# Two weight blocks in one walk over the normed tiles, and four quarter products moved ahead of the first scores

## The chip, the cores and the metric

The kernel runs on one core of one Trainium2 chip. The metric is the device time of one execution in microseconds (us); lower is better.

## The reference, cut to what matters

The program computes a mixer block with five branches and then a second block of two layers. The change sits in the first layer of the second block, an mLSTM over 512 tokens of 1024 features, 8 heads, float32:

```python
hn = rmsnorm(x, norm1_w[layer]) * (1 + scale1) + shift1
proj = h @ w_in
qk = jax.nn.silu(causal_conv(proj[..., :2 * M_QK], conv_w, conv_b))
v, o = ...                      # values and output gate, 1024 columns each
i_pre = IGATE_CAP * jnp.tanh(i_pre / IGATE_CAP)      # 8 columns of proj, one a head
lf = jax.nn.log_sigmoid(f_pre)                       # 8 more columns
# per head: scores q k^T times exp of gate differences, cumulated over time,
# times v, divided by max(|row sum|, exp(-m)), rms-normed, times sigmoid(o)
```

## The kernel before

Activations lie with features on the partitions: `m.HN` is 8 tiles of 128 features by 512 tokens. The weight matrix of this stage has 24 blocks of 128 columns, each 8 tiles deep, loaded by SP into a ring of 8 slots. Every engine has an instruction list of its own, written out by hand; engines wait for each other through semaphores only.

The order of the blocks is `M_BLOCKS`: q0 and k0 first, then 11 pairs (q1 k1, v0 v1, o0 o1, q2 k2, v2 v3, o2 o3, q3 k3, v4 v5, ...). The pairs are multiplied by a scheme with seven quarter products instead of eight, in the order P1, P7, P6, P2, P5, P4, P3: products of half tiles, of sums of inputs (`S1` to `S4`, made on DVE by `combine_inputs`) and of differences of weights (`T1` to `T4`, made on GpSimd). The results gather in PSUM banks 0, 1 and 5; between products ACT copies partial sums out (`keep`, L466), and a later product waits for that copy: P6 for the copy of P1, P5 for that of P6, P3 for that of P5. In all there are 77 quarter products, numbered 0 to 76; number n is product n mod 7 of pair n div 7. `M_AHEAD` of them are issued ahead of the first scores; after the scores of head h come `M_BESIDE[h]` more.

TensorE's list of the stage is thus: products of ones (`keep_busy`, L266, nothing reads them); a walk over the tiles of `m.HN` as ACT hands them over (L1777), with the 8 tiles of the gate columns (bank 4) and of block q0 (bank 0); block k0 (bank 1); the first seven quarter products; a transpose of the gate row; the other products ahead; then for each head its scores (L1692), from head 2 on the column sums for the variance of head h - 2 (in `Norm.var`, which waits for `norm_sq`), four quarter products, the weighted sums of the head before (`totals`, L1656 to L1661), and the other quarter products.

ACT's list begins with the tiles of `m.HN`, the copy of q0 out of its bank (`take`, L1738), tanh, exp and ln for the gates (L1781 to L1783, behind `gate_in`), the copy of k0, and then one `keep` for each quarter product in their order. The first P1 waits for the copy of q0, the first P7 for that of k0:

```python
if j == 0:
    pe.wait_ge(m.evac, self.plan.done + self.first - 1)      # P1; P7: self.first
```

Within a head, ACT's extra work stands at fixed indices n of the head's list of products: the root of a variance (`M_ROOT`), the silu of two convolved blocks (`M_CONV`), the square of a head's result (`M_SQUARE`), the decays of the next head in two halves (`M_DECAY`, `M_DECAY2`; for head 0 after n = 0 and n = 1). The blocks of an o pair go through a sigmoid when their last product is done (`take_pair`, L1746 to L1750). Scores of head h wait for the silus of blocks q and k of index h div 2. Functions of different tables make ACT load a table in between (ACT_TABLE_LOAD).

DVE makes HN with the layer norm's tiles, the sums of inputs, the gate rows (L1942 to L1959), the causal convolutions (L1905, L1907), and per head the weights, a division and the norm. GpSimd makes the weight differences and the last additions, and stores and spreads the gate rows by DMA.

Of the kernel before, what the change touches and what calls it, by code (L numbers as in the profile page):

```python
# [12 lines left out]
P = 128  # L13
# [3 lines left out]
KD = D // P  # L17
# [94 lines left out]
def rows(i, n):  # L112
    return slice(i * n, (i + 1) * n)
# [140 lines left out]
def in_strips(m, out, weights, act, start, stop, skip=False):  # L254

    columns = weights.shape[1]
    for at in range(0, columns, m.strip):
        part = slice(at, min(at + m.strip, columns))
        last = m.nc.tensor.matmul(out[part], weights[:, part], act, start=start, stop=stop, skip_group_check=skip)  # L259
    return last  # L260


def keep_busy(m, bank, n):

    for _ in range(n):
        m.nc.tensor.matmul(m.ps[:, bank, 0:P], m.ones[:], m.ones[:], start=True, stop=True)  # L266


def by_features(m, act, kt, ready=None):

    def block(bank, w):
        for k in range(kt):
            if ready:
                ready(k)
            last = in_strips(m, bank[:, 0:act.shape[2]], w[:, rows(k, P)], act[:, k, :], k == 0, k == kt - 1)
        return last
    return block
# [19 lines left out]
S3, S1, S2, S4 = range(1, 5)  # L297
# [290 lines left out]
class TokenNorm:  # L588
# [75 lines left out]
    def need(self, m, pe):  # L664
        return lambda k: pe.wait_ge(m.hn_ready, self.scaled + k + 1)


def give(eng, ins, sem, count, by=1):

    ins.then_inc(sem, by)  # L670
    eng.wait_ge(sem, count)
# [851 lines left out]
           (("o", 2), ("o", 3)), (("q", 3), ("k", 3)), (("v", 4), ("v", 5)), (("o", 4), ("o", 5)), (("v", 6), ("v", 7)),  # L1523
           (("o", 6), ("o", 7))]
M_BLOCKS = M_FIRST + [block for pair in M_PAIRS for block in pair]
M_AHEAD, M_BESIDE, M_TOTALS = 12, [8, 9, 9, 10, 9, 9, 8, 3], 4
M_ROOT, M_CONV = [None, None, 0, 0, 0, 0, 0, 0], [None, 6, None, 1, None, 1, None, None]
M_DECAY, M_DECAY2 = [6, 3, 3, 6, 3, 3, 2, None], [7, 4, 4, 7, 4, 8, 4, None]
M_SQUARE = [None, 7, 7, 8, 7, 7, 6, 2]
# [2 lines left out]
def out_piece(m, pe, plan, act_in, b, ks, kt=KD):  # L1532

    s = b % SLOTS
    if ks[0] == 0:
        pe.wait_ge(m.loaded[s], 16 * (plan.uses[s] + b // SLOTS + 1))
    for k in ks:
        last = in_strips(m, m.ps[:, b % BANKS, :], m.ring[:, s, rows(k, P)], act_in[:, k, :], k == 0, k == kt - 1)
    if ks[-1] == kt - 1:
        last.then_inc(m.blocks_done, 1)  # L1540
# [51 lines left out]
def stage_m(m):  # L1592


    nc, A, W, ps = m.nc, m.A, m.W, m.ps
    plan, out = m.plans["m_in"], m.plans["m_out"]
# [36 lines left out]
    with nc.Block() as block:  # L1633
        @block.sync
        def _(sp):
            load_rest(m, sp, plan)
            load_first(m, sp, out)
            load_rest(m, sp, out)
            load_first(m, sp, m.plans["ffn_up"], SLOTS, SLOTS // 2)
            load_first(m, sp, m.plans["ffn_up"], SLOTS // 2)  # L1640

        @block.tensor
        def _(pe):
            go = lambda n: pairs.multiply(pe, n)

            def totals(h):

                pe.wait_ge(prob_ready, h + 1)
                pe.wait_ge(m.evac, out_of("v", h))
                if h:  # L1650
                    pe.wait_ge(m.norm_in, norms[h - 1].in_k)
                    pe.wait_ge(m.norm_std, norms[h - 1].k)
                else:
                    pe.wait_ge(cT_out, 1)
                for i in range(ST):
                    last = nc.tensor.matmul(ps[:, 7, i * P:], values[:, h, rows(i, P)], probs[h % 2][:, i, i * P:],  # L1656
                                            start=(i == 0), stop=(i == ST - 1))
                last.then_inc(summed, 1)
                pe.wait_ge(keys_added, (ST - 1) * (h + 1))
                nc.tensor.matmul(ps[:, 6, 0:P], m.ones[:], probs[h % 2][:, 0, 0:P], start=True, stop=True)  # L1660
                nc.tensor.matmul(ps[:, 6, P:], m.ones[:], key_sum[:, h % 2, :], start=True,  # L1661
                                 stop=True).then_inc(counted, 1)

            need = norm_in.need(m, pe)
            keep_busy(m, 0, 12)
            pe.wait_ge(m.loaded[0], 16 * (plan.uses[0] + 1))
            for k in range(KD):
                need(k)
                last = nc.tensor.matmul(ps[0:32 + HEADS, 4, :], m.gates_w[:, k, :], m.HN[:, k, :], start=(k == 0),
                                        stop=(k == KD - 1))  # L1670
                if k == KD - 1:
                    last.then_inc(gates, 1)
                last = nc.tensor.matmul(ps[:, 0, :], m.ring[:, 0, rows(k, P)], m.HN[:, k, :], start=(k == 0),
                                        stop=(k == KD - 1))
            last.then_inc(m.blocks_done, 1)
            pe.wait_ge(m.loaded[1], 16 * (plan.uses[1] + 1))
            by_features(m, m.HN, KD)(ps[:, 1, :], m.ring[:, 1, :]).then_inc(m.blocks_done, 1)
            go(7)
            pe.wait_ge(c_ready, 1)
            for t in range(ST):  # L1680
                last = nc.tensor.transpose(ps[:, 6, rows(t, HEADS)], g["i"][:, rows(t, P)],
                                           m.c("ident")[0:HEADS, 0:HEADS])
            last.then_inc(cT_ready, 1)
            go(M_AHEAD - 7)

            for h in range(HEADS):
                lo = 64 * (h % 2)
                if h:
                    pe.wait_ge(prob_ready, h)
                pe.wait_ge(conv_out, 2 * (h // 2 + 1))  # L1690
                for i in range(ST):
                    last = nc.tensor.matmul(scores[i], qk_tile("k", h // 2)[lo:lo + 64, rows(i, P)],  # L1692
                                            qk_tile("q", h // 2)[lo:lo + 64, i * P:], start=True, stop=True)
                last.then_inc(score, 1)
                if h >= 2:
                    norms[h - 2].pe(m, pe)
                ahead = min(M_TOTALS, M_BESIDE[h])
                go(ahead)
                if h:
                    totals(h - 1)  # L1700
                go(M_BESIDE[h] - ahead)
                if h == HEADS - 1:
                    pe.wait_ge(head_out, EARLY)
                    pe.wait_ge(m.evac, plan.done + plan.n)
                    out_piece(m, pe, out, values, 0, range(0, EARLY))
            keep_busy(m, 1, 5)
            norms[HEADS - 2].pe(m, pe)
            keep_busy(m, 1, 8)
            totals(HEADS - 1)
            pe.wait_ge(m.evac, plan.done + plan.n)  # L1710
            out_piece(m, pe, out, values, 1, range(0, EARLY))
            out_piece(m, pe, out, values, 2, range(0, EARLY))
            norms[HEADS - 1].pe(m, pe)
            out_piece(m, pe, out, values, 3, range(0, EARLY))
            for b in range(4):
                for k in range(EARLY, HEADS):
                    pe.wait_ge(head_out, k + 1)
                    out_piece(m, pe, out, values, b, (k,))
            for b in range(4, out.n):
                pe.wait_ge(m.evac, out.done + b - BANKS + 1)  # L1720
                if b == out.n - 2:
                    out_piece(m, pe, out, values, b, range(0, KD // 2))
                    unnormed.bias_of(m, pe)
                    out_piece(m, pe, out, values, b, range(KD // 2, KD))
                else:
                    out_piece(m, pe, out, values, b, range(KD))
            unnormed.product(m, pe, 0, 2)
            norm_out.stat_of_sums(m, pe)
            unnormed.product(m, pe, 2, UNNORMED)
            norm_out.spread(m, pe)  # L1730
# [167 lines left out]
        def _(dve):  # L1898
# [38 lines left out]
            inputs = lambda which: combine_inputs(m, dve, nc.vector, m.HN, pairs.sums, pairs.past["inputs"], which)  # L1937
            dve.wait_ge(m.hn_ready, norm_in.scaled + KD)
            inputs(S3)
            inputs(S1)  # L1940
            dve.wait_ge(gates, 1)
            step(nc.vector.tensor_scalar(g["i"], ps[0:HEADS, 4, :], m.p("mi_b")[0:HEADS, :], None, ALU.add))  # L1942
            step(nc.vector.tensor_copy(g["f"], ps[32:32 + HEADS, 4, :]))
            step(nc.vector.tensor_scalar(g["f"], g["f"], m.p("mf_b")[0:HEADS, :], None, ALU.add))
            give(dve, nc.vector.scalar_tensor_tensor(g["t"], g["f"], -1.0, g["f"], ALU.mult, ALU.max), gate_in, 1)
            inputs(S2)
            inputs(S4)
            dve.wait_ge(gate_soft, 1)
            step(nc.vector.scalar_tensor_tensor(g["t"], g["f"], 0.0, g["t"], ALU.min, ALU.subtract))
# [26 lines left out]
            for h in range(HEADS):  # L1976
                dve.wait_ge(decay, h + 1)
                dve.wait_ge(score, h + 1)
                for i in range(ST):
                    last = nc.vector.scalar_tensor_tensor(probs[h % 2][:, i, i * P:], scores[i], 0.125, dec[:, i, i * P:],  # L1980
                                                          ALU.mult, ALU.mult)
# [1596 lines left out]
```

## Time and profile before

| what | value |
|---|---|
| median of 3 runs | 1947.34 us (1946.88 to 1947.86) |
| profiled execution, its own time | 1949.36 us |
| its span | 1947.4 us |
| mLSTM stage, first instruction on PE | 313.96 us |
| busy: PE, DVE, ACT, POOL | 1913.6, 869.7, 566.9, 680.9 us |
| HBM traffic over the span | 160 GB/s |

Times in the rows are microseconds from the start of the span of this one execution. A group of instructions of one kind is a row; its duration runs from the first start to the last end, and since matmuls are pipelined that end overlaps the start of the next row by some 0.1 to 0.2 us. So one step's length is best read from start to start. A float32 matmul shows as two instructions. PEclk is TensorE's granted clock, 1.00 for 2.4 GHz and 0.50 for 1.2 GHz.

### The profile page before, as it was taken

The numbers are of one execution on the slowest core, as the hardware profiler recorded it, in microseconds if no ns is written. First come the engines' busy times: TensorE is split into PE (matmuls) and PEld (weight loads), VectorE is DVE, ScalarE is ACT, GpSimd is POOL, SyncE is SP. The second block draws the span as 40 slices with busy tenths as digits, with TensorE's granted clock in tenths as the row PEclk, the third lists the DMA queues.
The fourth block names the chain that finished last, engine by engine and source line by source line (L and its number), as shares of the span: only waits on it lengthen the run. The fifth ranks groups of instructions, "written<-read, shape, count | busy, mean of one in ns | idle before, by whom it ended". The sixth has DMA issues, their size and how long they took to land. (4 is left out here: it accounts for less than half of the span.)

```text
span 1947.4 us, 36158 instructions
## 1 busy us (share of the span) xinstructions
PE 1913.6 (98%) x14812; PEld 1596.7 (82%) x14812; DVE 869.7 (45%) x1177; ACT 566.9 (29%) x1210; POOL 680.9 (35%) x590
## 2 busy tenths in 40 slices
PE   9999999999999999999999999999999999999997
PEld 8778645888746888888877888745999999999996
DVE  4898587667425444444436777732200000000023
ACT  1443213455512111110036657532120210111102
POOL 5755432655414444444526777520300000000011
PEclk9999999999999999999999999999999999999999
DMA  9214750322224666631211111101967578778893
GB/s 334 86 55 154 281 186 22 101 83 73 82 65 152 215 216 212 211 130 60 102 67 67 67 66 64 59 12 48 313 214 254 195 243 268 257 263 334 334 353 146
DMA packets 82822, 313.54 MB, mean 161 GB/s; under 512 B 10122, under 2 KB 10642, under 8 KB 82530
## 3 DMA queue, kind: packets, MB, share of 16 engines
q1 hardware_dynamic: 75952, 289.73, 42.2%
q0 software_dynamic: 4464, 14.35, 2.1%
q10 hardware_dynamic: 2241, 7.14, 1.0%
q8 instruction: 120, 1.97, 0.4%
q14 instruction: 45, 0.36, 0.1%
HBM read 301.43 MB, written 9.75 MB: 160 GB/s over the span
## 5 line engine op out<-in xcount | busy, mean ns | idle before, releaser
L259 PE MATMUL banks<-sb_act,sb_ring 128*64 128x112 f32 (+10 forms) x5184 | 686.1, 318 | 1.9 <-DMA sb_ring<-in_w_moe_up 1.0
L259 PEld LDWEIGHTS banks<-sb_act,sb_ring 128*128 128x128 f32 (+1 forms) x5184 | 598.9, 173 | 80.1 <-issue 66.5
L259 PE MATMUL banks<-sb_x_norm,sb_ring 128*128 128x256 f32 (+3 forms) x1616 | 330.9, 403 | 3.2 <-ACT sb_ring L466 2.3
L259 PEld LDWEIGHTS banks<-sb_x_norm,sb_ring 128*128 128x128 f32 (+1 forms) x1616 | 242.6, 171 | 66.0 <-issue 29.6
L3455 DVE TENSOR_TENSOR sb_act<-sb_work,banks 128x192 f32<-128x192 f32 (+7 forms) x88 | 27.2, 309 | 485.4 <-PE banks L259 478.3
L441 POOL TENSOR_TENSOR sb_ring<-sb_ring 128x512 f32<-128x512 f32 x146 | 206.4, 1414 | 104.7 <-PE banks L259 54.3
L259 PE MATMUL banks<-sb_work,sb_ring 128*128 128x256 f32 (+2 forms) x1028 | 220.6, 410 | 1.9 <-ACT sb_ring L466 1.8
L259 PEld LDWEIGHTS banks<-sb_work,sb_ring 128*128 128x128 f32 (+1 forms) x1028 | 147.9, 168 | 53.2 <-issue 32.7
L2986 POOL DMA_INDIRECT sb_work<-first_expert_rows,sb_table x8 | 7.5, 936 | 441.6 <-DMA first_expert_rows<-sb_x_norm 439.5
L3257 ACT ACTIVATE sb_work<-banks 128x192 f32<-128x192 f32 (+7 forms) x88 | 25.7, 294 | 296.4 <-PE banks L259 294.4
L497 POOL TENSOR_TENSOR sb_act<-sb_act,sb_ring 128x256 f32<-128x256 f32 x75 | 71.8, 958 | 69.4 <-ACT sb_act L466 61.9
L2150 ACT ACTIVATE sb_work<-banks 128x256 f32<-128x256 f32 x84 | 32.2, 383 | 216.9 <-PE banks L259 216.9
L259 PEld LDWEIGHTS banks<-sb_ring,sb_act 128*128 128x128 f32 (+3 forms) x1136 | 89.5, 155 | 5.0 <-issue 4.8
L259 PE MATMUL banks<-sb_ring,sb_act 128*128 128x128 f32 (+3 forms) x1136 | 92.0, 274 | 0.3 <-DVE sb_act L3455 0.3
L259 PE MATMUL banks<-sb_x_res,sb_ring 128*128 128x256 f32 (+2 forms) x362 | 90.7, 405 | 0.8 <-PEq L2045 0.5
L259 PE MATMUL banks<-sb_work 128*128 128x256 f32 (+1 forms) x528 | 91.5, 341 | 0.0
L695 DVE SCALAR_TENSOR_TENSOR sb_act<-sb_act,sb_cond 128x1024 f32<-128x1024 f32 x63 | 84.3, 1338 | 6.5 <-DMA sb_act<-in_cond_w 3.7
L259 PEld LDWEIGHTS banks<-sb_work 128*128 128x128 f32 (+1 forms) x528 | 74.5, 171 | 8.6
L259 PEld LDWEIGHTS banks<-sb_x_res,sb_ring 128*128 128x128 f32 (+1 forms) x362 | 66.3, 187 | 16.7 <-issue 8.7
L2194 POOL TENSOR_TENSOR sb_work<-sb_ring 128x512 f32<-128x512 f32 x21 | 26.6, 1267 | 147.6 <-PE banks L259 138.3
L259 PEld LDWEIGHTS banks<-sb_act 128*64 128x64 f32 (+1 forms) x1112 | 61.1, 142 | 15.0 <-issue 9.4
L466 ACT ACTIVATE sb_ring<-banks 128x256 f32<-128x256 f32 x114 | 42.3, 380 | 101.5 <-PE banks L259 101.0
(501 smaller groups left out, 2459.2 us busy)
## 6 DMA issues: line engine op xcount, KB each, us to landing
sb_ring<-in_w_moe_up SPq DMA_DIRECT2D x176, 512.0 KB, 4.9
sb_ring<-in_w_moe_down SPq DMA_DIRECT2D x64, 704.0 KB, 6.2
sb_act<-in_cond_w SPq DMA_DIRECT2D x84, 512.0 KB, 3.8
sb_ring<-in_w_ffn_up SPq DMA_DIRECT2D x44, 512.0 KB, 5.2
sb_ring<-in_w_h_in SPq DMA_DIRECT2D x32, 512.0 KB, 4.1
sb_ring<-in_w_in SPq DMA_DIRECT2D x28, 512.0 KB, 5.5
sb_ring<-in_w_m_in SPq DMA_DIRECT2D x24, 512.0 KB, 4.0
sb_ring<-in_w_ffn_down SPq DMA_DIRECT2D x16, 704.0 KB, 5.6
```

What stands on the lines that cost most here:

```text
L259: last = m.nc.tensor.matmul(out[part], weights[:, part], act, start=start, stop=stop, skip_group_check=skip)
L441: made = lambda a, b, out: give(pool, m.nc.gpsimd.tensor_tensor(out, a, b, ALU.subtract), m.combined, self.weights_no(j, which))
L466: copy = lambda out, bank: m.nc.scalar.activation(out, self.halves(bank), ACT.Copy).then_inc(m.partials, 1)
L497: made = lambda out, x, y: give(eng, engine.tensor_tensor(self.halves(out), x, y, ALU.add), m.added, self.added_no(j, which))
L695: step(m.nc.vector.scalar_tensor_tensor(out, src, w, out, ALU.mult, ALU.add))
L2150: nc.scalar.activation(part, bank(j, i), ACT.Copy).then_inc(partials, 1)
L2194: made = lambda a, b, out, n: give(pool, nc.gpsimd.tensor_tensor(out, a, b, ALU.subtract), combined, weights_no(j, n))
L2986: nc.gpsimd.indirect_dma_start(got[2 * t + j], None, table, bass.IndirectOffsetOnAxis(ap=m.table[:, c:c + 1], axis=0)).then_inc(got_sem[2 ...
L3257: nc.scalar.activation(silu_t[j % 2][:, 0:cap], ps[:, 2 * j % BANKS, 0:cap], ACT.Silu).then_inc(silu, 1)
L3455: nc.vector.tensor_tensor(hid[:, j, 0:cap], silu_t[j % 2][:, 0:cap], ps[:, (2 * j + 1) % BANKS, 0:cap], ALU.mult).then_inc(m.evac, 2)
```

## The change

Block k0 joins the walk: each normed tile is multiplied with the gate columns, q0 and k0. Three products of ones stand ahead of the walk instead of twelve. Sixteen quarter products come ahead of the first scores instead of twelve, and heads 1, 2, 3 and 4 have one less beside them (8, 8, 9 and 8; head 0 keeps 8). On DVE the sum S2 is made ahead of the gate rows instead of behind them. The lists of ACT's extra work keep their indices.

```diff
-M_AHEAD, M_BESIDE, M_TOTALS = 12, [8, 9, 9, 10, 9, 9, 8, 3], 4
+M_AHEAD, M_BESIDE, M_TOTALS = 16, [8, 8, 8, 9, 8, 9, 8, 3], 4
...
-            keep_busy(m, 0, 12)
-            pe.wait_ge(m.loaded[0], 16 * (plan.uses[0] + 1))
+            keep_busy(m, 0, 3)
+            for b in range(2):
+                pe.wait_ge(m.loaded[b], 16 * (plan.uses[b] + 1))
             for k in range(KD):
                 need(k)
                 last = nc.tensor.matmul(ps[0:32 + HEADS, 4, :], m.gates_w[:, k, :], m.HN[:, k, :], start=(k == 0),
                                         stop=(k == KD - 1))
                 if k == KD - 1:
                     last.then_inc(gates, 1)
-                last = nc.tensor.matmul(ps[:, 0, :], m.ring[:, 0, rows(k, P)], m.HN[:, k, :], start=(k == 0),
-                                        stop=(k == KD - 1))
-            last.then_inc(m.blocks_done, 1)
-            pe.wait_ge(m.loaded[1], 16 * (plan.uses[1] + 1))
-            by_features(m, m.HN, KD)(ps[:, 1, :], m.ring[:, 1, :]).then_inc(m.blocks_done, 1)
+                for b in range(2):
+                    last = nc.tensor.matmul(ps[:, b, :], m.ring[:, b, rows(k, P)], m.HN[:, k, :], start=(k == 0),
+                                            stop=(k == KD - 1))
+                    if k == KD - 1:
+                        last.then_inc(m.blocks_done, 1)
             go(7)
...
             inputs(S3)
             inputs(S1)
+            inputs(S2)
             dve.wait_ge(gates, 1)
...
             give(dve, nc.vector.scalar_tensor_tensor(g["t"], g["f"], -1.0, g["f"], ALU.mult, ALU.max), gate_in, 1)
-            inputs(S2)
             inputs(S4)
```

## Rows read from the trace of the kernel before

**Rows 1.** The page: busy time of TensorE, its share of the span, instructions.

```profile
PE 1913.6 (98%) x14812; PEld 1596.7 (82%) x14812; DVE 869.7 (45%) x1177; ACT 566.9 (29%) x1210; POOL 680.9 (35%) x590
```

**Rows 2.** Timeline of PE, 312 to 345 us: start, duration, engine, line, operation, tiles, count, idle before.

```profile
313.96 2.92 PE L266 MATMUL banks<-sb_ones 128*128 128x128 f32 x24 [1.71 <-PEq L1275]
316.81 1.05 PE L1669 MATMUL banks<-sb_x_norm,sb_gates_w 128*40 128x512 f32 x2
...
318.84 1.05 PE L1669 MATMUL banks<-sb_x_norm,sb_gates_w 128*40 128x512 f32 x2
...
334.85 8.76 PE L259 MATMUL banks<-sb_x_norm,sb_ring 128*128 128x512 f32 x24
```

**Rows 3.** Timeline of ACT, 312 to 345 us.

```profile
314.74 0.72 ACT L1777 ACTIVATE sb_x_norm<-sb_x_norm,sb_mod 128x512 f32<-128x512 f32 x1
...
335.05 0.60 ACT L1738 ACTIVATE sb_act<-banks 128x512 f32<-128x512 f32 x1 [2.20 <-PE banks L1673]
...
338.12 0.63 ACT L1781 ACTIVATE sb_work<-sb_work 8x512 f32<-8x512 f32 x1 [1.17 <-DVE sb_work L1945]
...
339.43 1.28 ACT L1783 ACT_TABLE_LOAD   x1
340.73 0.72 ACT L1783 ACTIVATE sb_work<-sb_work,sb_cst 8x512 f32<-8x512 f32 x1
341.98 0.60 ACT L1738 ACTIVATE sb_act<-banks 128x512 f32<-128x512 f32 x1 [0.53 <-PE banks L259]
```

**Rows 4.** Timeline of DVE, 312 to 345 us.

```profile
332.88 2.48 DVE L321 TENSOR_TENSOR sb_act<-sb_x_norm 128x1024 f32<-128x1024 f32 x2 [0.79 <-ACT sb_x_norm L1777]
335.41 0.74 DVE L1942 TENSOR_SCALAR sb_work<-banks,sb_par 8x512 f32<-8x512 f32 x1
```

**Rows 5.** Timeline of PE in the loop over the heads.

```profile
343.44 3.62 PE L259 MATMUL banks<-sb_act,sb_ring 128*128 128x256 f32 x16
...
373.71 1.97 PE L259 MATMUL banks<-sb_act,sb_ring 128*128 128x256 f32 x8 [0.69 <-ACT sb_ring L466]
...
398.51 1.89 PE L259 MATMUL banks<-sb_act,sb_ring 128*128 128x256 f32 x8
...
402.11 2.42 PE L1692 MATMUL banks<-sb_act 64*128 64x512 f32 x8
...
424.60 2.42 PE L1692 MATMUL banks<-sb_act 64*128 64x512 f32 x8
...
438.07 1.89 PE L259 MATMUL banks<-sb_x_norm,sb_ring 128*128 128x256 f32 x8
...
443.25 1.89 PE L259 MATMUL banks<-sb_x_norm,sb_ring 128*128 128x256 f32 x8
...
448.52 2.42 PE L1692 MATMUL banks<-sb_act 64*128 64x512 f32 x8
```

**Rows 6.** Timeline of ACT in the loop over the heads.

```profile
400.40 1.48 ACT L1768 ACTIVATE sb_act<-sb_act,sb_par 128x512 f32<-128x512 f32 x2
...
430.24 1.28 ACT L565 ACT_TABLE_LOAD   x1
...
433.18 1.28 ACT L1768 ACT_TABLE_LOAD   x1
...
436.38 1.28 ACT L1746 ACT_TABLE_LOAD   x1
...
438.60 0.63 ACT L1750 ACTIVATE sb_act<-sb_act 128x512 f32<-128x512 f32 x1
...
449.11 0.62 ACT L561 ACTIVATE sb_work<-sb_act 128x512 f32<-128x512 f32 x1
```

**Rows 7.** Windows: busy time (instructions) of five engines, PEclk, DMA share, GB/s.

```profile
1349.00:1349.50 0.50, 0.00 (x0) 0.00 (x0) 0.17 (x1) 0.00 (x0) 0.00 (x0) 0.79 0.00 0
1352.50:1353.00 0.50, 0.50 (x6) 0.50 (x5) 0.40 (x3) 0.13 (x1) 0.00 (x0) 0.80 0.00 0
```

**Rows 8.** Timeline of PE, 1240 to 1262 us, the longest gap behind the prologue.

```profile
1252.29 0.69 PE L259 MATMUL banks<-sb_act 128*64 128x64 f32 x16 [2.05 <-issue]
```

## The prediction

> **What bounds the kernel now.** I read the page first: TensorE is busy for 98% of the span [rows 1]. Idle time on PE is scarce, so an edit moves the end by what it adds to or takes from PE's queue: instructions, or waits. The second view was the timeline of PE from the start of the mLSTM stage, 313.96 us: twelve products of ones, the walk (gates and q0, tile by tile), block k0 and the first quarter product P1, all of it L259 in one group, then P7 [rows 2, 5]. Each time I then read the timeline of the engine that PE will have to wait for, ACT and DVE in the same stretch [rows 3, 4]. Last came the loop over the heads, where PE has one visible gap, 0.69 us before the P6 at 373.71 [rows 5], and the chain on ACT that sets its margins [rows 6].
>
> **The front: what is saved.** Twelve products of ones take 2.85 us (313.96 to 316.81), 0.237 each [rows 2]; nine fewer give PE 2.1 us. The first normed tile is ready at 315.46 (314.74 + 0.72 on ACT) [rows 3], so the walk starts at 315.5 instead of 316.81. One tile of gates and q0 takes 2.03 us (316.81 to 318.84). Eight products of k0 and the four of P1 run from 334.85 to 343.44, 8.59 us [rows 2, 5]. Three quarter products and a small change-over take 5.27 us (443.25 to 448.52), so one takes 1.73 [rows 5]; k0 is then 6.86, or 0.86 a tile. A tile of the new walk takes 2.03 + 0.86 = 2.89 us. The last tile is ready by 332.9, when DVE takes it up [rows 4]; the walk gets to it at 315.5 + 7 x 2.89 = 335.7, so it no longer waits for tiles. It ends at 315.5 + 8 x 2.89 = 338.7; k0 used to end at 341.7. That is 3.0 us won, if PE can go on.
>
> **The front: what is late next.** It can't go on for long. P1 writes bank 0 and needs q0 copied out; P7 writes bank 1 and needs k0 copied out. ACT copies q0, then waits for the gates' tanh, exp and ln, and only then copies k0. Before, PE was the late one: ACT waited 0.53 us for k0 [rows 3]. Now the gates of the last tile are done at 315.5 + 7 x 2.89 + 1.05 = 336.8, not at about 334. DVE turns them into the input of tanh in 338.12 - 335.41 = 2.71 us [rows 3, 4], so 339.6. q0's last product ends one product later, about 1.1, at 337.9; ACT copies it (0.60) until 338.5 and loads a table (1.28) until 339.85; the tanh starts there. From the tanh to the end of ln took 3.33 us (338.12 to 340.73 + 0.72) [rows 3]: ln ends at 343.2, k0's copy at 343.8, and P7 starts about 0.15 later, at 343.95. It started at 343.44 [rows 5]. P1 ends at 340.4, so PE stands idle for 3.5 us, and the 3.0 us won come back as **0.5 us lost**. The addition S2, moved ahead of the gates (two such take 2.48 us), ends at 336.6, before the gates come: free [rows 4]; had the gates come at 334, it would have cost up to 1.2. The rest of DVE's gate work, behind the ln, shifts by 1.7 us (ln ends at 343.2, not 341.45), and with it the rows that GpSimd stores and spreads and the first convolutions; their readers are the decays and scores of head 0, which come four products (7 us) later than before: covered. Without that cover it would cost up to 1.7. On SP the reload of q0's slot goes out 3 us later and that of k0's 3 us earlier; pair 3, which reads them, is more than 20 products of 1.73 us off.
>
> **The heads.** The number of quarter products is the same (16 + 61 = 12 + 65), and from head 5 on every instruction stands where it stood. Only stalls count. ACT's extras (root, silu, decays, square) stand at fixed indices in each head's list, and the lists of heads 1 to 4 have lost one product each.
> - Head 0. The old stall goes: P6 had waited behind the decays. Copy, decays, copy, decays, copy takes from 443.25 to 449.21 (the square at 449.11 overlaps that copy) [rows 6], 5.96 us after its first product ended. P3 of pair 2 now needs the third copy (0.15 more to start), and PE is there after three products, 5.2: 0.9 lost for 0.7 gained, **+0.2**.
> - Scores of head 2. They need the silu of q1 and k1, placed after index 6 of head 1. That product ended at 398.51 and the silu at 400.40 + 1.48 = 401.88, 3.37 later; two more products brought PE to 402.11 [rows 5, 6]. Now one product follows: PE is there about 1.9 after, the silu 3.37, with 0.15 to start: **+1.6**.
> - Head 3. Its list now begins with (P4, P3) of an o pair. ACT does the copy, root, sigmoid take, silu and then the copy that P6 of pair 6 needs. From the scores' start: the root's load at 5.64 (430.24 - 424.60), root 2.65 (load to load 2.94 less the copy between), take 2.85 (436.38 to 438.60 + 0.63), silu load and two silus 2.8 (1.28 + 1.48), copy 0.4, start 0.15, in all 14.45 [rows 5, 6]. PE is there after 13.47 (424.60 to 438.07): **+1.0**.
> - Variance of head 2, after the scores of head 4. The square ended 6.48 us after P6 (443.25 to 449.73) [rows 6]; between them stand the same copies and decays. PE has one product less to go: from P6 to the scores it took 5.27, now 3.55, plus 2.4 of scores, so it is there at 5.95, and 0.1 goes by before it starts: **+0.65**.
> DVE's division and convolutions in these heads have one product, 1.7 us, less until their reader; four products lie between, and I take them as covered. Sum: 0.5 + 0.2 + 1.6 + 1.0 + 0.65 = 4.0 us.
>
> **The clock.** The 3.5 us gap is longer than any in the trace: after the longest behind the prologue, 2.05 us, the clock stayed [rows 8]. At 1349.3 it fell to half, in a stretch where PE did nothing for half a microsecond, and at 1352.7 it was back, 3.4 us later [rows 7]. A fall costs half of the busy time it covers: 0 to 1.7 us for such a fall, 3.4 if it lasts twice as long. The products after the gap are dense; some of the fall may lie in the gap. I take 1.5. I think it somewhat likelier than not, since this gap is seven times that half microsecond, and none as long is seen to leave the clock alone. By the Trainium skill (TensorE: Matmul & The Clock Gate, HAM oscillation) a wait inside a loop sets the clock back and each dense burst after it starts at half rate; that speaks for the fall and against this edit. The trace agrees that it falls around idle PE and shows no gap of this size.
>
> A second rule of the skill speaks against it too: by ScalarE: Activation LUTs (What ACT_TABLE_LOAD costs) each switch of tables costs a drain of 1.38 us beside the 1.28 us of load. The trace has the load at 339.43 and the ln at 340.73, 1.30 later [rows 3], so no drain is on this path; with it, three loads at head 3 would make that stall an estimated 4.1 us longer than by the rows.
>
> **Rivals.** (a) The same stalls, the clock kept: +4.0 us, 1951.3. For it: the clock held after 2.05 us [rows 8]. Against it: this gap is nearly twice as long. (b) The clock falls at the start of the walk as well, since three products of ones and 0.8 us idle replace twelve: 1.5 to 1.7 more, 1954.4. For it: the gap of 1.71 us ahead of the ones [rows 2] stays; against it: no gap there reaches 2.05. (c) Some of the head stalls are milder, because the fixed order on ACT has more slack than I count; without the two smaller ones, and with the clock kept: 4.0 - 1.65 = +2.35, 1949.7. For it: two of the three margins are summed from six or seven steps. (d) Not slower: k0's copy doesn't stand behind the ln. Then P7 starts at 340.4, 3.0 earlier, and with the head stalls it comes to -3.0 + 3.45 = +0.45, 1947.8; with those hidden as well 1944.3, 0.15% less. It decides at a gate chain that ends before 339.9. Against it: the order on ACT is written out, and ACT's own row shows k0 taken right after it. (e) The edit doesn't buy what it says even there: tiles of 2.89 us are no bargain if the walk then ends no earlier than the gate chain; this is part of my own forecast.
>
> **Numbers.** The profiled execution took 1949.36 us, 1.96 of it outside the span of 1947.4; the median of the runs is 1947.34, 2.02 lower. The sum, 4.0 + 1.5 = 5.5, gives 1954.9 for such an execution and **1952.8** for the median. Chances: forecast 0.42, (a) 0.33, (b) 0.07, (c) 0.13, (d) 0.05. A measurement of this kernel tells 0.2% from no change, 3.9 us or 1951.2. Case (a) lies on that line, I give half of it to each side: slower 0.66, same 0.32, faster 0.02. The range reaches from (c) at 1949.4, a little under its sum, to (b) with some of its fall, 1954.9; the forecast's own is 1951.3 to 1953.2 (0 to 1.7 for the fall, and 0.2 for the stalls).
>
> **What would show it.** In the profile after: the first gates matmul at 315.5 and gates and both blocks every 2.9 us; PE idle for 3.5 us before P7, put down to ACT's copy of k0; that copy right behind the ln at 343.2; PEclk under 1.00 between 340 and 350 (absent in (a)). Then gaps of about 1.6 before the scores of head 2, 1.0 before a P6 in head 3, 0.65 before a variance, 0.9 in head 0. The prediction is wrong if P7 starts before 343, if the scores of head 2 don't wait, or if the DMA of the gate rows lands so late that DVE holds up the decays, which I took as covered.

## The result, and the profile after

The changed kernel takes 1956.45 us (median of 6 runs, 1955.77 to 1962.62) against 1947.6 for the kernel before on the same chip (6 runs, 1946.64 to 1948.87): ratio 1.0045, interval 1.0035 to 1.0056, or 8.8 us more. Timed again later it was 1.0038 (1.0025 to 1.0051), 7.4 us more. (Here and below "more" or "over before" is the ratio less one, times the median of before; the difference of the medians themselves can be up to 1 us off it, 8.0 for the second timing.) Forecast were 5.5 more, with a range up to 1954.9. The direction was right; the size lies outside the range.

The profiled execution took 1956.7 us, its span is 1954.4, 7.0 more than before. The page gives nearly the same busy times as [rows 1]:

```profile
PE 1913.8 (98%) x14794; PEld 1594.6 (82%) x14794; DVE 869.9 (45%) x1177; ACT 567.2 (29%) x1210; POOL 680.7 (35%) x590
```

Nine fewer products of ones take nine instruction pairs off PE (14812 - 14794 = 18), and yet its busy time didn't fall. The timeline of PE, changed kernel, from the start of the stage, answers to [rows 2, 5]:

```profile
312.34 0.91 PE L266 MATMUL banks<-sb_ones 128*128 128x128 f32 x6 [1.71 <-PEq L1275]
313.99 1.02 PE L1670 MATMUL banks<-sb_x_norm,sb_gates_w 128*40 128x512 f32 x2 [0.74 <-ACT sb_x_norm L1778]
314.94 1.98 PE L1675 MATMUL banks<-sb_x_norm,sb_ring 128*128 128x512 f32 x4
...
334.24 1.05 PE L1670 MATMUL banks<-sb_x_norm,sb_gates_w 128*40 128x512 f32 x2
...
337.12 1.97 PE L259 MATMUL banks<-sb_x_norm,sb_ring 128*128 128x256 f32 x8
342.38 5.38 PE L259 MATMUL banks<-sb_act,sb_ring 128*128 128x256 f32 x16 [3.30 <-ACT sb_act L1739]
347.60 1.89 PE L259 MATMUL banks<-sb_x_norm,sb_ring 128*128 128x256 f32 x8
...
381.30 2.00 PE L259 MATMUL banks<-sb_act,sb_ring 128*128 128x256 f32 x8 [0.68 <-ACT sb_act L466]
...
409.86 2.64 PE L1693 MATMUL banks<-sb_act 64*128 64x512 f32 x8 [1.62 <-ACT sb_act L1769]
412.42 2.07 PE L259 MATMUL banks<-sb_work,sb_ones 128*128 128x512 f32 x2
...
446.38 1.97 PE L259 MATMUL banks<-sb_act,sb_ring 128*128 128x256 f32 x8 [1.09 <-ACT sb_ring L466]
...
458.16 1.13 PE L259 MATMUL banks<-sb_work,sb_ones 128*128 128x512 f32 x2 [0.56 <-ACT sb_work L561]
```

Five waits stand in brackets behind P1: P7's for the copy of k0, head 0's (as long as before), the scores of head 2, a P6 in head 3, and the variance of head 2. And two rows are longer than their work: P7 and P6 take 5.22 us from start to start (342.38 to 347.60) where two products take 3.45, and the two column sums at 412.42 show 2.07 where they show 1.13 at 458.16.

The timeline of ACT, changed kernel, gives the causes of the four new waits; it answers to [rows 3, 6]:

```profile
336.38 0.60 ACT L1739 ACTIVATE sb_act<-banks 128x512 f32<-128x512 f32 x1 [5.15 <-PE banks L1675]
...
338.29 0.63 ACT L1782 ACTIVATE sb_work<-sb_work 8x512 f32<-8x512 f32 x1
...
340.89 0.72 ACT L1784 ACTIVATE sb_work<-sb_work,sb_cst 8x512 f32<-8x512 f32 x1
341.64 0.60 ACT L1739 ACTIVATE sb_act<-banks 128x512 f32<-128x512 f32 x1
...
408.24 1.47 ACT L1769 ACTIVATE sb_act<-sb_act,sb_par 128x512 f32<-128x512 f32 x2
...
445.85 0.66 ACT L466 ACTIVATE sb_ring<-banks 128x256 f32<-128x256 f32 x2
...
457.48 0.62 ACT L561 ACTIVATE sb_work<-sb_act 128x512 f32<-128x512 f32 x1
```

The copy of k0 no longer waits for PE; it comes right behind the ln, without idle time. The silus that the scores need end at 409.71 (408.24 + 1.47), and the scores start 0.15 later. The copy at 445.85 is the one that P6 of head 3 waits for, and the square at 457.48 ends 0.06 before the variance starts. DVE took up the gates of the last tile with 0.39 us of idle time, so S2 ahead of them cost nothing; this row of DVE's timeline answers to [rows 4]:

```profile
335.40 0.74 DVE L1944 TENSOR_SCALAR sb_work<-banks,sb_par 8x512 f32<-8x512 f32 x1 [0.39 <-PE banks L1670]
```

Now the clock, in windows of 2 us of the changed kernel (columns as in [rows 7]):

```profile
344.00:346.00 2.00, 2.00 (x6) 1.57 (x5) 1.93 (x3) 0.38 (x1) 0.00 (x0) 0.50 0.00 0
...
412.00:414.00 2.00, 2.00 (x5) 1.03 (x4) 1.30 (x3) 0.00 (x0) 1.84 (x3) 0.50 0.51 111
...
1256.00:1258.00 2.00, 0.39 (x13) 0.42 (x15) 1.85 (x5) 1.96 (x3) 0.35 (x1) 1.00 0.39 154
1258.00:1260.00 2.00, 2.00 (x17) 0.87 (x14) 1.90 (x3) 0.07 (x1) 1.47 (x2) 0.59 0.01 4
```

Half clock (1.2 GHz) holds from 343.6 to 347.0, from 411.9 to 415.3 and from 1258.4 to 1261.8, each time behind a gap on PE: 3.30, 1.62 and 2.05 us. The last gap is the one of [rows 8]; in the trace of before the windows behind it are at 1.00. One fall near 1350 [rows 7] is in both kernels.

By stage, changed kernel (windows from the start of the stage to P7, to the scores of head 0, to those of head 5, to the end of the stage, to the end):

```profile
312.34:342.38 30.04, 26.01 (x62) 8.82 (x63) 25.79 (x31) 16.41 (x23) 8.60 (x6) 1.00 0.09 35
342.38:371.10 28.72, 28.72 (x180) 25.96 (x180) 15.10 (x20) 10.06 (x20) 17.69 (x19) 0.94 0.27 79
371.10:476.47 105.37, 101.42 (x535) 82.69 (x534) 69.69 (x80) 56.37 (x110) 59.34 (x63) 0.98 0.24 78
476.47:601.16 124.69, 124.35 (x496) 78.74 (x495) 51.02 (x63) 46.05 (x77) 38.11 (x40) 1.00 0.23 78
601.16:1954.40 1353.24, 1330.47 (x11894) 1171.17 (x11894) 475.16 (x744) 349.04 (x788) 393.71 (x310) 1.00 0.50 176
```

The kernel before, same cuts (second and third taken together):

```profile
313.96:343.44 29.48, 27.79 (x80) 11.07 (x81) 26.82 (x33) 16.26 (x22) 8.60 (x6) 1.00 0.07 23
343.44:471.16 127.72, 127.02 (x716) 106.73 (x714) 83.51 (x99) 66.87 (x131) 76.70 (x81) 1.00 0.25 85
471.16:595.85 124.69, 124.35 (x496) 78.70 (x495) 51.06 (x62) 45.52 (x76) 37.95 (x40) 1.00 0.24 78
595.85:1947.40 1351.55, 1328.95 (x11894) 1170.71 (x11894) 474.60 (x744) 348.95 (x788) 394.18 (x310) 1.00 0.50 176
```

To P7 0.56 us more; from P7 to the scores of head 5 6.37 more (28.72 + 105.37 - 127.72); from there to the stage's end nothing; after the stage 1.69 more, one fall behind the 2.05 us gap; and the stage begins 1.62 earlier (312.34 for 313.96). Together 7.0. The stage itself is 288.82 us long for 281.89: 6.93 more. That is what this pair of traces shows of the change; the gap ahead of the fall behind the stage is in the kernel before too, so that those 1.69 us are chance.

The other 1.8 of the 8.8 us are not in this pair of traces. The profiled execution of before took 1949.36, 1.8 above the median of its runs; that of after lies 0.25 above its own. Before's prologue holds a clock fall of 6.8 us (304.8 to 311.6), after's one of 3.4; half of the difference is about the 1.62 us by which before's stage began later. This fall lasted 6.8 us in all six traces of kernels built on the kernel before and in two of the eight built on the changed one (3.4 in the other six); why is not known, and that it sets before's profiled execution apart from its other runs is argued, not shown.

### The profile page after: what moved, and what is told of

Same layout as the page of the kernel before. It is cut to its first block and busy times, and to the rows that moved or that the text cites. A ratio compares the mean times of both kernels' runs of the same rounds, so it can differ in the third digit from the quotient of the medians.

```text
span 1954.4 us, 36117 instructions
## 1 busy us (share of the span) xinstructions
PE 1913.8 (98%) x14794; PEld 1594.6 (82%) x14794; DVE 869.9 (45%) x1177; ACT 567.2 (29%) x1210; POOL 680.7 (35%) x590
## 5 line engine op out<-in xcount | busy, mean ns | idle before, releaser
L259 PE MATMUL banks<-sb_x_norm,sb_ring 128*128 128x256 f32 (+2 forms) x1600 | 326.0, 404 | 3.4 <-ACT sb_ring L466 2.3
```

## The experiments

The theory after the result: the change costs 3.5 us of waits by ACT's order, and the gaps it opens put the clock at risk, at 1.7 us for a fall of 3.4 us and twice that for one of 6.8. Rivals: the clock falls by themselves wherever they like (then waits alone matter and falls average out); the walk itself is dearer than it looks; or the waits move on when one is removed.

This table holds the results and what was read from the fourteen traces; the median of the kernel before stands beside each, taken in the same session on the same chip, so that only ratios compare across sessions. "Stage" runs from the first product of ones to the stage's end, "falls" are those within it, "rest" is the stage less half of the time at half clock.

```
kernel            median   before's  ratio (interval)          stage   falls us   rest
before (trace)                                                 281.89    0       281.9
after             1956.45  1947.6    1.0045 (1.0035 to 1.0056) 288.82    6.8     285.4
after_again       1956.13  1948.09   1.0038 (1.0025 to 1.0051) 288.82    6.8     285.4
ones_in_gap       1958.96  1951.82   1.0039 (1.0025 to 1.0052) 287.18    3.4     285.5
k0_first          1960.49  1951.82   1.0043 (1.0030 to 1.0057) 291.75   13.6     285.0
gates_split       1956.65  1951.82   1.0030 (1.0019 to 1.0041) 287.62    3.4     285.9
act_places        1953.6   1951.82   1.0012 (1.0003 to 1.0021) 285.21    6.8     281.8
ahead_only        1953.88  1948.09   1.0026 (1.0016 to 1.0035) 288.14    6.8     284.7
walk_only         1952.55  1948.09   1.0021 (1.0012 to 1.0030) 285.43    3.4     283.7
ones3_only        1949.4   1948.09   1.0007 (0.9998 to 1.0016) 281.88    0       281.9
ones_both_gaps    1953.25  1948.45   1.0025 (1.0014 to 1.0036) 287.09    3.4     285.4
all_moved         1948.88  1948.45   1.0003 (0.9994 to 1.0012) 281.39    0       281.4
part_walk         1945.32  1948.45   0.9983 (0.9974 to 0.9992) 279.60    0       279.6
part_walk_decays  1945.32  1948.45   0.9985 (0.9976 to 0.9994) 278.64    0       278.6
```

**ones_in_gap.** The changed kernel, with products of ones in the gap ahead of P7:

```diff
-            go(7)
+            go(1)
+            keep_busy(m, 7, 14)
+            go(6)
```

> The changed kernel with 14 products of ones (3.3 us) on bank 7 between the first P1 and P7; every wait stays. If the fall of the clock at 343.7 is paid because TensorE stands idle ahead of P7, it disappears and the kernel is 1.7 us faster than the changed one, about +7.1 us against the kernel before. If the fall has another cause, or costs nothing because P7's successors wait anyway: no change, +8.9. If the ones delay P7 itself: slower by up to 0.3.

P7's gap shrank to 0.18 us and no fall came behind it, nor behind the scores' gap; but one came at the start of the walk, 315.5 to 318.9. Rest 285.5, as for the changed kernel: the waits are untouched, and what the filled gap can spare is the fall only. Ratio 1.0039, 7.6 us over before, for 8.8 and 7.4 of the changed kernel: no gain that the measurement can tell.

**k0_first.** The changed kernel, the copy of k0 ahead of the gate chain on ACT:

```diff
             take("q", 0)
+            take("k", 0)
             act.wait_ge(gate_in, 1)
...
-            take("k", 0)
             for i in range(4):
```

> The changed kernel, but ACT copies k0 ahead of tanh, exp and ln. P7 then starts at 338.9 instead of 342.4. My theory: the next copy, that of P1, still stands behind the ln, so P6 waits for it until about 343 (2.5 us of idle time, now ahead of P6), and only 1.0 us is won, 2.7 if the clock holds over the shorter gap: +6.2 to +7.9 us against the kernel before. Rival: the copy of k0 is the whole of the wait; then 3.3 + 1.7 = 5.0 us are won, +3.9.

P7 goes on at once, but the wait moves on to the P6 behind it, since the copy of P1 now stands behind the ln, and a second wait appears at the P6 of the next pair (v0 v1), behind GpSimd's last additions. Timeline of PE, k0_first:

```profile
345.86 1.97 PE L259 MATMUL banks<-sb_act,sb_ring 128*128 128x256 f32 x8 [2.22 <-ACT sb_ring L466]
...
359.70 2.02 PE L259 MATMUL banks<-sb_ring,sb_act 128*128 128x128 f32 x16 [0.87 <-ACT sb_ring L466]
```

2.22 + 0.87 is 3.09, for 3.30 before the move. Here the rival that the wait moves on is right: ACT's chain sets the front, in whatever order PE meets it. Of the 1.0 us that was expected to be won the stage shows 0.4 (rest 285.0 for 285.4) and the time nothing (1.0043). No fall came behind the 2.22 us gap in this trace; falls stand at the start of the walk (313.2 to 320.0) and behind the scores' gap.

**gates_split.** The same, and the copy of P1 (`keep(0, 0)`) between the exp and the ln, so that P6 finds it:

```diff
             step(nc.scalar.activation(g["t"], g["t"], ACT.Exp, scale=-1.0))
+            keep(0, 0)
             give(act, nc.scalar.activation(g["t"], g["t"], ACT.Ln, bias=m.c("one")[0:HEADS, :]), gate_soft, 1)
...
-            for i in range(4):
+            for i in range(1, 4):
```

> The changed kernel, but ACT's order is copy of q0, copy of k0, tanh, exp, copy of P1, ln, the other copies. Neither P7 nor P6 has the ln ahead of it: P6 waits 0.5 us at most. Theory: 3.0 us of the front and the 1.7 us of the clock come back, 4.7 won, +4.2 us against the kernel before. Rival: the later gate row moves the wait to the transposes or the first scores: then less than 2 us is won.

Timeline of PE, gates_split:

```profile
349.32 1.97 PE L259 MATMUL banks<-sb_act,sb_ring 128*128 128x256 f32 x8 [1.32 <-ACT sb_act L466]
...
357.15 2.02 PE L259 MATMUL banks<-sb_ring,sb_act 128*128 128x128 f32 x16 [1.75 <-ACT sb_ring L466]
```

The gap splits into 1.32, ahead of P3, and 1.75, ahead of the P6 of the next pair: 3.07 again. Timeline of ACT, gates_split, for the two causes:

```profile
348.13 0.63 ACT L1790 ACTIVATE sb_work<-sb_work 8x512 f32<-8x512 f32 x1 [1.86 <-DVE sb_work L1960]
...
356.35 0.38 ACT L1747 ACTIVATE sb_act<-banks 128x256 f32<-128x256 f32 x1 [6.90 <-POOL sb_act L497]
```

ACT stops for DVE's gate rows and later for GpSimd's last additions; behind both stand copies that PE needs. In this trace there is no half clock in the front, and the ratio is 1.0030 (5.8 us) for 1.0045 and 1.0038 of the changed kernel, though the intervals overlap. The expectation, a gain of 4.7 us, was wrong.

**act_places.** The changed kernel, ACT's extras re-placed for the shorter lists:

```diff
-M_ROOT, M_CONV = [None, None, 0, 0, 0, 0, 0, 0], [None, 6, None, 1, None, 1, None, None]
-M_DECAY, M_DECAY2 = [6, 3, 3, 6, 3, 3, 2, None], [7, 4, 4, 7, 4, 8, 4, None]
+M_ROOT, M_CONV = [None, None, 0, 0, 0, 0, 0, 0], [None, 2, None, 3, None, 1, None, None]
+M_DECAY, M_DECAY2 = [6, 3, 3, 4, 3, 3, 2, None], [7, 4, 4, 6, 4, 8, 4, None]
```

> The changed kernel with four indices of ACT's extra work moved: silu of head 1 from 6 to 2, of head 3 from 1 to 3, decays of head 3 from 6 and 7 to 4 and 6. Theory: the gaps of 1.62, 1.09 and 0.56 us go, 3.3 us, and with the first of them the fall of the clock at 411.9 (1.4 us): 4.7 won, +4.2 us against the kernel before. Rival: falls of the clock don't hang on the gaps: 3.3 won, +5.6. Second rival: the gaps only move to other copies: under 1.5 won.

The waits of 1.62, 1.09 and 0.56 us are gone, and so is the fall behind the scores: windows of act_places, 345 to 349 us (P7's gap, still there) and 410 to 414 us (the scores):

```profile
345.00:347.00 2.00, 1.86 (x6) 1.55 (x7) 1.80 (x3) 0.27 (x1) 0.00 (x0) 0.75 0.00 0
347.00:349.00 2.00, 2.00 (x6) 1.64 (x5) 1.93 (x3) 0.38 (x1) 0.00 (x0) 0.50 0.00 0
410.00:412.00 2.00, 2.00 (x12) 1.40 (x12) 0.01 (x1) 0.90 (x2) 1.06 (x2) 1.00 0.00 0
412.00:414.00 2.00, 2.00 (x9) 1.30 (x8) 0.53 (x1) 0.00 (x0) 1.69 (x3) 1.00 0.05 18
```

Rest 281.8 for 285.4: 3.6 us, of which the waits are 3.27. The time goes from 8.8 and 7.4 us over the kernel before to 2.3. The head stalls with the fall behind them are thus the larger part of the loss.

**ahead_only, walk_only, ones3_only.** The kernel before, with one part of the change each: only `M_AHEAD, M_BESIDE`; only the walk with both blocks and S2 ahead of the gates; only `keep_busy(m, 0, 3)`.

> The kernel before with 16 products ahead and the shorter lists of heads 1 to 4 alone. Theory: the head gaps are the edit's own and don't need the new front: 1.6, 1.1 and 0.6 us, with the fall of the clock behind the first of them 4.7: +3.3 to +4.7 us against the kernel before. Rival: they come from the front's delay of the gate rows; then within 1 us of before.

> The kernel before with k0 in the walk and S2 moved, but twelve products of ones and 12 ahead. Theory: the gates of the last tile come 1.3 us later than with three products of ones, at 24.2 us of the stage, P7 at about 31.3 instead of 29.5, with 3.3 us idle ahead of it: +1.8 by the delay, +3.5 with a fall of the clock. Rival: the walk itself is sound and only the shorter run of ones spoils the clock; then +0.5 at most.

> The kernel before with three products of ones instead of twelve. The walk begins 1.3 us earlier but ends with the last tile, as before: 0 us. If the clock falls at the walk's start in some executions, its 1.7 us lie mostly in the 1.7 us that the walk waits for tiles: up to +0.5 in the median. Rival: falls at the walk's start cost all of their 1.7 to 3.4 us.

Measured 5.1, 4.1 and 1.4 us over before. ahead_only has all the head stalls (0.68, 1.63, 1.09, 0.56) and a fall of 6.8 us behind the second. walk_only has P7's gap (3.30), a fall behind it, and no new wait in the heads. Fewer ones alone: no wait and no fall in the stage, and its 1.4 us are within the noise (interval 0.9998 to 1.0016). The first two lie 0.4 and 0.6 us above the upper ends of what was expected. The three sum to 10.6 for 7.4 to 8.8 together. In the traces the three products of ones pay only together with the walk: to P7 walk_only takes 31.27 us (313.86 to 345.13), the full change 30.04, the kernel before 29.48.

**after_again.** The changed kernel once more, unaltered, to see whether its falls repeat.

> The changed kernel unchanged, beside the other three on one chip. Theory: its loss is that of the parts, +3.3 to +4.7 from the heads and about +2.3 to +4 from the front and its clock: +8.9 us as before. The three gaps of the heads and the 3.3 us ahead of P7 stand at the same places; where the clock falls may differ.

The stage is as long as before to a hundredth, 288.82 us, and yet its falls are others. Windows of after_again:

```profile
344.00:346.00 2.00, 2.00 (x11) 1.77 (x10) 1.93 (x3) 0.38 (x1) 0.00 (x0) 1.00 0.00 0
...
410.00:412.00 2.00, 2.00 (x7) 1.27 (x5) 0.00 (x0) 0.00 (x0) 1.83 (x4) 0.50 0.37 113
```

Behind the same 3.30 us gap ahead of P7 the clock stayed, and behind the 1.63 us gap ahead of the scores it was low for 6.8 us (408.7 to 415.6) instead of 3.4. Whether a fall comes differs from execution to execution of one kernel; the places where falls came are few, and the same in these traces.

**ones_both_gaps.** ones_in_gap, and seven more products of ones in the gap of the scores:

```diff
+                if h == 2:
+                    keep_busy(m, 2, 7)
                 pe.wait_ge(conv_out, 2 * (h // 2 + 1))
```

> The changed kernel with products of ones in two gaps: 14 ahead of the first P7, 7 (1.66 us) on bank 2 ahead of the scores of head 2. All waits stay. Theory: falls of the clock behind these two gaps are a part of the loss of their own; without them the stage lasts 1.7 to 5 us less than in the changed kernel's profiles (288.8 us), nearest 285.2, which is before's 281.9 plus the waits of 3.8, less 0.5: and the time is +4 to +5.5 us against the kernel before, not +7.4 to +8.9. Rival: the falls come whatever stands in the gaps.

Windows of ones_both_gaps:

```profile
315.00:317.00 2.00, 2.00 (x3) 0.84 (x3) 1.93 (x3) 1.37 (x2) 0.00 (x0) 0.50 0.00 0
342.00:344.00 2.00, 1.82 (x15) 1.66 (x15) 0.78 (x2) 1.81 (x4) 0.00 (x0) 1.00 0.13 51
...
410.00:412.00 2.00, 2.00 (x9) 1.31 (x8) 0.03 (x1) 0.30 (x1) 1.69 (x3) 1.00 0.00 0
412.00:414.00 2.00, 2.00 (x14) 1.52 (x14) 1.90 (x4) 0.00 (x0) 1.70 (x3) 1.00 0.43 131
```

Full clock behind both filled gaps, the work as late as in the changed kernel (rest 285.4), and 4.9 us over before for 8.8 and 7.4, as expected; its interval (1.0014 to 1.0036) still overlaps that of the second timing. One fall came at the start of the walk again.

Every execution, profiled or not, also has its mean granted clock on record, to three digits. One less that clock, times the span, is what half clock takes from it (an estimate, good to about half a microsecond as a mean over a kernel's executions, and taken as if PE were dense). So the extra time over before splits into clock and the rest: after_again 3.1 and 4.3, ones_both_gaps 1.1 and 3.5, ahead_only 2.3 and 3.0, walk_only 2.1 and 2.3, ones3_only 1.5 and -0.1, act_places 2.3 and -0.1. With ones in both gaps most of the clock's part is gone and the waits stay; fewer ones alone cost, as far as they cost anything, by the clock.

**all_moved.** gates_split and act_places in one, and head 0's decays all ahead of its first copy:

```diff
+            decays(0, 0, ST)
             for h in range(HEADS):
...
-                    if h == 0 and n < 2:
-                        decays(0, 2 * n, 2 * n + 2)
```

> The changed kernel with ACT's order around the gates split, its four indices moved and the decays of head 0 made ahead of the loop. Left are the waits for the gate rows that the split order brought out (1.3 and 1.75 us ahead of P3 and of the next P6). Theory: front +1.0, heads -0.7, no gap over 2 us: +0.3 us against the kernel before, within 1.5. Rival: the four products moved ahead cost something that no gap shows; then over +2.

Only the waits of 1.32 and 1.76 in the front are left, no fall in the stage; stage 281.39, and the time is that of the kernel before (1.0003). So with the head stalls gone the new layout comes out even; what it would be worth without the 3.1 us of waits that are left in the front was not tested.

**part_walk, part_walk_decays.** The kernel before, where the walk only fills what PE would idle: three tiles of k0 ahead of tiles 5, 6 and 7, the other five behind the walk, six products of ones, and the gate rows on DVE ahead of S1 and S2.

```diff
-            keep_busy(m, 0, 12)
-            pe.wait_ge(m.loaded[0], 16 * (plan.uses[0] + 1))
+            keep_busy(m, 0, 6)
+            for b in range(2):
+                pe.wait_ge(m.loaded[b], 16 * (plan.uses[b] + 1))
             for k in range(KD):
+                if k >= 5:
+                    of_k0(k - 5, k - 4)
                 need(k)
...
             last.then_inc(m.blocks_done, 1)
-            pe.wait_ge(m.loaded[1], 16 * (plan.uses[1] + 1))
-            by_features(m, m.HN, KD)(ps[:, 1, :], m.ring[:, 1, :]).then_inc(m.blocks_done, 1)
+            of_k0(3, KD).then_inc(m.blocks_done, 1)
...
             inputs(S3)
-            inputs(S1)
             dve.wait_ge(gates, 1)
...
+            inputs(S1)
             inputs(S2)
```

`of_k0(a, b)` multiplies tiles a to b - 1 of k0 into bank 1. part_walk_decays also makes all of head 0's decays ahead of its first copy, by the edit shown for all_moved.

> The kernel before with six products of ones, three of k0's eight tiles in the walk, where it waited for tiles 5, 6 and 7, and the gate rows ahead of S1 and S2 on DVE; the gates of the last tile come as early as before (20.0 us into the stage), P7 at 27.2 instead of 29.5. Theory (the gate chain sets the front): -2.3 us against the kernel before. Rival (the gates' reader DVE or GpSimd binds soon after): under 1 us won.

> The same with the decays of head 0 ahead of the loop over the heads, where ACT is idle: the gap of 0.69 us ahead of P6 in head 0 goes as well: -3.0 us against the kernel before.

Timeline of PE, part_walk:

```profile
332.55 1.05 PE L1678 MATMUL banks<-sb_x_norm,sb_gates_w 128*40 128x512 f32 x2
...
334.50 4.46 PE L1666 MATMUL banks<-sb_x_norm,sb_ring 128*128 128x512 f32 x10
338.79 1.89 PE L259 MATMUL banks<-sb_x_norm,sb_ring 128*128 128x256 f32 x8
340.71 3.69 PE L259 MATMUL banks<-sb_act,sb_ring 128*128 128x256 f32 x16
```

The last gates come 18.96 us after the stage's start (332.55 - 313.59), in the kernel before 18.95, in the changed kernel 21.90 (334.24 - 312.34). k0's five remaining tiles and P1 cover the gate chain on ACT, and P7 starts at 27.12 with no gap, for 29.48 before and 30.04 after. The stage takes 279.60, 2.3 less than before, and the time is 3.3 us less (ratio 0.9983, interval 0.9974 to 0.9992): faster than both kernels. Of the 1.0 us that the stage doesn't hold, the granted clocks of the executions give 0.8 (an estimate as above). No run separates the three changes (k0's tiles in the walk, fewer ones, DVE's order). Moving head 0's decays as well removes its 0.70 us wait in the trace (278.64), but the time can't tell the two apart.

## Why the prediction was right and wrong

**Front.** Right. Less the 1.62 us by which the whole stage came earlier, the walk was to begin at 313.9, the last gates at 334.1, the tanh at 338.2 and P7 at 342.3; they came at 313.99, 334.24, 338.29 and 342.38. The gap was 3.30 for 3.5 and the loss 0.56 for 0.5. k0's copy came right behind the ln. S2 was free. (Two of the sums on the way are 0.1 high, 338.7 for the walk's end and 339.6 for tanh's input; nothing later hangs on them.) k0_first and gates_split show that the whole of ACT's chain is the cause and not the place of one copy: both move the wait, neither removes it.

**Head 0.** Wrong by the little that was at stake: the new wait was to be 0.9 for 0.7, and it is 0.68 for 0.69. The wait moved to another product at the same length. A part of the 0.2 was never there: the 0.9 is a difference of starts, the 0.7 the idle time in brackets; from start to start the old wait is 0.85 us (373.71 less 371.13, the start of the product ahead of it, less 1.73).

**Scores of head 2, P6 of head 3, variance.** Right: 1.62, 1.09 and 0.56 for 1.6, 1.0 and 0.65. act_places shows that the fixed places are their cause. The other estimate for head 3, 4.1 us more by a drain at each switch of tables, did not come: the silus there start 1.30 us after the start of their table's load (443.04 to 444.34), and the wait is 1.09. DVE's work in these heads was covered, as taken.

**Sum of the waits.** 3.27 new us in the heads and 0.56 in the front make 3.83 for 4.0. The stage less its falls grew by 3.5; where the missing 0.3 went is not followed up.

**The clock.** This term of the sum failed: 1.5 us for one fall behind P7's gap, and nothing for the three new gaps in the heads. In the stage of the changed kernel it measured 3.4 us. The step behind it was the sentence that the longest gap so far, 2.05 us, left the clock alone [rows 8], read as if shorter gaps were harmless. [rows 7] spoke against that reading: the fall there stands at an idle time of 0.61 us. What it cost where it fell, 1.7 to 1.8 (5.22 - 3.45), was right. But it fell behind the gap of 1.62 us too (2.56 + 1.87 + 2.26 for 2.35 + 0.96 + 1.79 from start to start, 1.6 us; 3.4 in after_again), and behind the old 2.05 us gap, whose clock had been seen to hold in a single trace. With two falls in the stage and one behind it: 3.5 + 3.4 + 1.7 - 1.6 (the earlier start) = 7.0, the difference of the spans. Over all traces of kernels that have the change's parts, the falls at each of these places cost on average, as half of the time at half clock: behind P7's gap 1.3 us (10 us in four traces), behind the scores' gap 2.3 (27 us in six), at the start of the walk behind three ones 0.9 (17 us in nine). With the 3.5 of the waits that gives an estimated 8.0 us, between the 7.4 and the 8.8 measured. It leaves out the prologue's fall, which was the shorter one in most traces of the changed layout; the granted clocks of all executions give less for the clock, 3.1.

Against the rival that falls come by themselves wherever they like stand the places: in the stage there was none in the three traces that had none of these gaps and starts, behind P7's gap one in 3 of 4 traces, behind the scores' gap in 5 of 6, and with ones in the gaps none (two traces for P7's, one for the scores'). The filled gaps alone would be thin evidence, since a fall came at the walk's start in both of those traces; with act_places and the clocks of all executions it is good, not complete.

**The rivals.** (a), the clock kept, would have given 1951.3 and was farther off than the forecast. (b) had a fall at the walk's start: not in the changed kernel's two traces, but in four of the seven other traces with three ones ahead of the walk. The step "no gap there reaches 2.05" was wrong for the same reason as above. (c) is refuted by the head stalls, (d) by ACT's row. (e) named the weak point of the edit: part_walk, which gains, keeps the gates as early as before, and the full walk delays them by 2.9 us. That this is why it gains is read from the traces; its three changes were not tried one by one.

**What stays open.** Why a given gap brings a fall in one execution and none in another, and why some gaps never do; why the prologue's fall was shorter in most traces of the changed layout; why the medians differ by 1.8 more than the spans; and why the three parts sum to more than the whole, which their intervals allow.

## What to carry to other kernels

Before you move work ahead of others' waits, ask what source feeds the longest serial chain on another engine: fill idle time with the moved work, but keep that source as early as it was. Places of extra work given as indices into a list must be set anew when the list gets shorter. And price a new gap on a dense TensorE as the wait plus a chance of a clock fall, for gaps under 2 us too, give a kernel several traces before you call a gap safe, and never read one trace in which the clock held as a rule.

## What the runs showed of the hardware

I hadn't expected falls behind so short gaps. Over the traces of this case, the clock went to half behind the 1.62 us gap ahead of the scores in 5 of 6 traces where it stood unfilled, and in none of those without that gap or with ones in it. Behind the 3.30 us gap ahead of P7 it fell in 3 of 4 (after, act_places, walk_only; not after_again). At the start of the walk, with three products of ones ahead of it, in 4 of 9; with six or twelve in none of 5. And behind the same 2.05 us gap near 1255 us it fell in 9 traces of 14. This row of PE's timeline in the changed kernel is that gap, the same as in [rows 8]:

```profile
1257.61 0.69 PE L259 MATMUL banks<-sb_act 128*64 128x64 f32 x16 [2.05 <-issue]
```

The length of a gap doesn't decide. In 13 of 14 traces the clock fell at the gap of 0.61 us near 1350 us, within 1.3 us of its end at the latest, and it never fell behind the gap of 1.12 or 1.13 us near 1290 us (0 of 14), nor behind the 1.09 us ahead of P6 in head 3 (0 of 7), nor in the two traces with gaps of 1.32 and 1.75 us in the front. Timeline of PE, kernel before, the first two of these:

```profile
1290.78 2.40 PE L259 MATMUL banks<-sb_work,sb_act 128*64 128x128 f32 x40 [1.12 <-ACT sb_act L568]
...
1349.54 3.48 PE L3031 MATMUL banks<-sb_cst,sb_x_res 128*128 128x128 f32 x16 [0.61 <-PEq L2410]
```

From the prologue on, the falls lasted 3.4 or 6.8 us, nothing between, but for the one that runs over the kernel's end; so one costs 1.7 or 3.4 us where PE is dense. The four traces of the session in which before's median was 1951.82 (1947.6 to 1948.45 elsewhere) have one more near 1885 us, which no other trace has; so compare a kernel only with the kernel before on the same chip. By the Trainium skill (TensorE: Matmul & The Clock Gate, A second HAM failure mode: psum-queue depth-cycling) short idles between groups of matmuls, repeated often enough, can also make the clock swing. The traces agree that short gaps are enough; here they are single ones, the 1.62 us ahead of the scores among them, and not each of them brings a fall.
